# Delta rule, triangular inverse: odd chunks through the two other quarters of TensorE's array

## The reference, cut to what matters

```
def gated_delta_chunked(q, k, v, g, beta, s0):
    ...
    decay = jnp.exp(jnp.where(incl, g[..., :, None] - g[..., None, :], -jnp.inf))
    m = jnp.where(strict, jnp.einsum('bhnid,bhnjd->bhnij', k_beta, k) * decay, 0.0)
    t_inv = lax.linalg.triangular_solve(m + eye, ..., left_side=True, lower=True, unit_diagonal=True)
    u = jnp.einsum('bhnij,bhnjd->bhnid', t_inv, v * beta[..., None])
    w = jnp.einsum('bhnij,bhnjd->bhnid', t_inv, k_beta * jnp.exp(g)[..., None])
```

## Time and profile before

| | us |
|---|---|
| median of 3 runs | 4217.92 (4216.91 to 4218.13) |
| the profiled execution | 4220.12 |
| its span | 4218.3 |
| PE busy in the span | 3938.0 (93%) |
| DVE, ACT, POOL busy | 1680.2, 851.4, 692.3 |
| mean granted TensorE clock | 0.964 of full |

### The profile page before, as it was taken

The page is one execution under the profiler, slowest core; times in us unless marked ns, Lnnn a source line. Parts: engine busy times, 40 slices in busy tenths (PEclk is TensorE's granted clock), DMA queues, the critical chain, the costliest instruction groups (busy, mean ns, idle before and its releaser), DMA issues. The chain is left out here.

```text
span 4218.3 us, 51374 instructions
## 1 busy us (share of the span) xinstructions
PE 3938.0 (93%) x20867; PEld 2405.2 (57%) x20867; DVE 1680.2 (40%) x3134; ACT 851.4 (20%) x1663; POOL 692.3 (16%) x513
## 2 busy tenths in 40 slices
PE   7998889999999999899998999989998898999988
PEld 4565445554448666488745677768654444443333
DVE  2337343323764554533474656634124324111111
ACT  3224320000121333200013333321113201000000
POOL 0003212222420111123342332310002200000000
PEclk9999999999999999899998999999989998999999
DMA  5107611112541100254352010014200314999999
GB/s 175 40 11 285 198 40 60 60 60 95 170 126 56 46 31 26 93 217 160 111 173 50 26 31 26 19 39 154 63 0 1 155 46 192 406 420 422 422 421 374
DMA packets 323233, 580.12 MB, mean 138 GB/s; under 512 B 58700, under 2 KB 189228, under 8 KB 322360
## 3 DMA queue, kind: packets, MB, share of 16 engines
q1 hardware_dynamic: 323000, 576.83, 37.3%
...
## 5 line engine op out<-in xcount | busy, mean ns | idle before, releaser
L3348 PE MATMUL dn_ps<-room,dn_w 128*128 128x512 f32 (+1 forms) x616 | 230.2, 520 | 0.5 <-DVE dn_v_tok L3897 0.3
L961 PE MATMUL ffn_up_ps<-ffn_up_t,room 128*128 128x384 f32 (+1 forms) x704 | 208.3, 440 | 8.0 <-DVE room L1037 8.0
L961 PE MATMUL ffn_up_ps<-room 128*128 128x384 f32 (+1 forms) x704 | 203.9, 433 | 0.0
L4907 PE MATMUL experts_ps<-experts_ring,experts_xs 128*64 128x512 f32 (+1 forms) x768 | 164.1, 580 | 21.9 <-DMA experts_ring<-in_w_up 21.9
L961 PEld LDWEIGHTS ffn_up_ps<-ffn_up_t,room 128*128 128x128 f32 x704 | 136.0, 194 | 66.1 <-DVE room L1037 9.5
L1233 PE MATMUL ffn_down_ps<-ffn_down_w_sums,ffn_w 128*128 128x512 f32 x330 | 163.1, 604 | 10.8 <-DVE ffn_down_w_sums L1321 10.8
L2637 PE MATMUL hgrn_ps<-room,hgrn_w 128*128 128x512 f32 x372 | 170.3, 593 | 0.9 <-DVE hgrn_v L2891 0.9
L4907 PE MATMUL experts_ps<-experts_ring,room 128*64 128x512 f32 (+1 forms) x768 | 161.1, 570 | 8.7 <-DMA experts_ring<-in_w_up 8.1
L961 PEld LDWEIGHTS ffn_up_ps<-room 128*128 128x128 f32 x704 | 134.0, 190 | 55.5
L1044 DVE TENSOR_TENSOR room<-ffn_up_ps,room 128x384 f32<-128x384 f32 (+1 forms) x154 | 73.4, 489 | 222.2 <-PE ffn_up_ps L961 222.2
L5001 DVE TENSOR_TENSOR x_sb<-x_sb,experts_ps 128x512 f32<-128x512 f32 x56 | 38.5, 688 | 297.9 <-PE experts_ps L4842 297.9
...
## 6 DMA issues: line engine op xcount, KB each, us to landing
experts_ring<-in_w_gate SPq DMA_DIRECT2D x128, 704.0 KB, 14.9
experts_ring<-in_w_up SPq DMA_DIRECT2D x128, 704.0 KB, 16.7
...
```

Of the source, the lines that this page charges most:

```text
L961: mm = nc.tensor.matmul(result(n, p), lhs[:, k, :], rhs[:, k, :], start=k == 0, stop=k == half - 1)
L3348: mm = nc.tensor.matmul(out, ahead.tile[:, k, :] if k < by_ahead else wt[:, h % 2, piece, k, :], hT[:, k, tok], start=k == 0, stop=k == KD ...
L4907: mm = nc.tensor.matmul(ps[out_rows, 3 * n + c, 0:b - a], xs_now[:, j, at:at + SLOTS], ring[:, w_at + a:w_at + b], start=j == 0, stop=j == ...
```

## The change

`Y` is split by the chunk's parity. For odd chunks the output of `y` goes to the other half of the partitions, and `d` and `dt` read `Y` and `LT` from there, so that odd chunks use the upper right and lower left quarters. Their output comes back to the right half. Even and odd chunks write to different banks: `y` to 2 and 3, `d` and `dt` to 3 and 4 (three chunks each, `dt` behind `d` in the bank).

To have the odd chunks' `LT` in the other half, DVE makes it (`crossed`: two instructions per level, one for each half, reading `W` in one half and writing `LT` in the other), straight after `place_w`. POOL makes the even chunks' `LT` only, half as much. `y` now waits for `place_w` of the level before (`w_cp`), since it writes into bank 3. `place_z` waits for the end of `dt`, where it waited for the end of `d`, and `d`'s own semaphore is gone. The copies into `T` at level 5 are four where they were two.

```diff
-        Y = sb("Y", TILES, BLOCK)
+        Y = sb("Y", 2, ODD, BLOCK)
...
+        def split_of(bank, side, c, after=0):
+            return ps[sides_of[side], bank + c % 2, (after + c // 2) * BLOCK:(after + c // 2 + 1) * BLOCK]
+        def half_at(side, c):
+            return side if c % 2 == 0 else 1 - side
...
                 if n == 0:
                     pe.wait_ge(S["y_out"], L * h)
+                    pe.wait_ge(S["t_off"], 2 * h)
+                pe.wait_ge(S["w_cp"], (L - 1) * h + n)
...
-                        mm = nc.tensor.matmul(block_of(2, to_side, c), neg_m[rows, c, sides_of[to_side]], R[rows, c, :], start=True, stop=True)
+                        mm = nc.tensor.matmul(split_of(2, half_at(to_side, c), c), neg_m[rows, c, sides_of[to_side]], R[rows, c, :], start=True, stop=True)
...
-                if n < L - 1:
-                    for c in range(TILES):
-                        for side, rows in enumerate(sides_of):
-                            mm = nc.tensor.matmul(block_of(3, side, c), LT[rows, c, :], Y[rows, c, :], start=True, stop=True)
-                    mm.then_inc(S["d_mm"], 1)
+                pe.wait_ge(S["lt_crossed"], 2 * (L * h + n + 1))
                 pe.wait_ge(S["w_cp"], (L - 1) * h + n)
...
+                if n < L - 1:
+                    for i in range(ODD):
+                        for c in (2 * i, 2 * i + 1):
+                            for side in range(2):
+                                rows = sides_of[half_at(side, c)]
+                                nc.tensor.matmul(split_of(3, side, c), LT[rows, c, :], Y[rows, c % 2, c // 2, :], start=True, stop=True)
+                    for i in range(ODD):
+                        for c in (2 * i, 2 * i + 1):
+                            for side in range(2):
+                                rows = sides_of[half_at(side, c)]
+                                mm = nc.tensor.matmul(split_of(3, side, c, ODD), Y[rows, c % 2, c // 2, :], LT[rows, c, :], start=True, stop=True)
+                    mm.then_inc(S["dt_mm"], 1)
+                    return
...
-                nc.gpsimd.tensor_tensor(LT[:, :, :], W[:, h % 2, :, :], small(SMALL_HALVES + n + 1), ALU.mult).then_inc(S["lt_done"], 1)
+                nc.gpsimd.tensor_tensor(LT[:, 0::2, :], W[:, h % 2, 0::2, :], small(SMALL_HALVES + n + 1, ODD), ALU.mult).then_inc(S["lt_done"], 1)
...
-                dve.wait_ge(S["d_mm"], (L - 1) * h + n + 1)
-                nc.vector.copy_predicated(Z[:, :, :], small_mask(n + 1), blocks(3)).then_inc(S["z_cp"], 1)
+                dve.wait_ge(S["dt_mm"], L * h + n + 1)
+                nc.vector.copy_predicated(by_parity(Z[:, :, :]), parity_mask(n + 1), split_blocks(0)).then_inc(S["z_cp"], 1)
...
+            def crossed(n, h):
+                if h is None or n == L:
+                    return
+                if n:
+                    dve.wait_ge(S["w_cp"], (L - 1) * h + n)
+                else:
+                    dve.wait_ge(S["w_start"], 2 * h + 2)
+                    if h:
+                        dve.wait_ge(S["dt_mm"], L * h)
+                for side, rows in enumerate(sides_of):
+                    nc.vector.tensor_tensor(LT[sides_of[1 - side], 1::2, :], W[rows, h % 2, 1::2, :], small(SMALL_HALVES + n + 1, ODD, rows), ALU.mult).then_inc(S["lt_crossed"], 1)
...
                 place_w(n, hi)
+                if n < L - 1:
+                    crossed(n + 1, hi)
+                else:
+                    crossed(0, hp)
```

More of the change, by code:

```diff
@@ L3164, in chunk @@
         return slice(at, at + P)
+    ODD = TILES // 2
     sides = []
@@ L3247, in delta_mixer @@
                                              "conv", "z_cp", "r_done", "w_cp", "w_start", "kk_out", "mt_done", "qk_out", "ssq_out", "ssk_out", "v_scaled", "b_done", "q_scaled", "rho", "s_done",
[L3248 removed]
+                                             "o_half", "o_done", "w_ident", "lt_done", "lt_crossed", "rhs_done", "b_wide", "qk_masked", "t_done", "t_off", "stored", "z_in*2", "z_mm", "z_taken", "z_stored*4", also=[ahead.sem]))
         def wide(first):
@@ L3267, in block_of, with split_blocks, by_parity, parity_mask @@
             return ps[sides_of[side], bank, c * BLOCK:(c + 1) * BLOCK]
-        def small(n):
-            return cst[:, HALVES + n // 2, n % 2 * BLOCK:(n % 2 + 1) * BLOCK].unsqueeze(1).broadcast_to([P, TILES, BLOCK])
+        def split_of(bank, side, c, after=0):
+            return ps[sides_of[side], bank + c % 2, (after + c // 2) * BLOCK:(after + c // 2 + 1) * BLOCK]
+        def split_blocks(after):
+            return ps[:, 3:5, after * BLOCK:(after + ODD) * BLOCK].rearrange("p o (c i) -> p o c i", c=ODD)
+        def by_parity(x):
+            return x.rearrange("p (c o) i -> p o c i", o=2)
+        def parity_mask(level):
+            n = SMALL_EITHER + level
+            rows = cst[:, HALVES + n // 2, n % 2 * BLOCK:(n % 2 + 1) * BLOCK]
+            return rows.bitcast(U32).unsqueeze(1).unsqueeze(1).broadcast_to([P, 2, ODD, BLOCK])
+        def half_at(side, c):
+            return side if c % 2 == 0 else 1 - side
+        def small(n, count=TILES, part=slice(0, P)):
+            return cst[part, HALVES + n // 2, n % 2 * BLOCK:(n % 2 + 1) * BLOCK].unsqueeze(1).broadcast_to([part.stop - part.start, count, BLOCK])
         def small_mask(level, part=slice(0, P)):
@@ L3426, in d_of @@
                     pe.wait_ge(S["t_off"], 2 * h)
+                if n < L - 1:
[11 more added lines that the diff above has]
+                    return
                 for c in range(TILES):
-                    for side, rows in enumerate(sides_of):
-                        to_side = side if n < L - 1 else 1 - side
-                        mm = nc.tensor.matmul(block_of(4, to_side, c), Y[rows, c, :], LT[rows, c, :], start=True, stop=True)
+                    for side in range(2):
+                        rows = sides_of[half_at(side, c)]
+                        mm = nc.tensor.matmul(split_of(3, 1 - side, c), Y[rows, c % 2, c // 2, :], LT[rows, c, :], start=True, stop=True)
                 mm.then_inc(S["dt_mm"], 1)
@@ L3823, in place_w @@
                 for d, rows in enumerate(sides_of):
-                    nc.vector.tensor_copy(T[rows, h % 2, d, :, sides_of[1 - d]], blocks(4)[rows, :, :]).then_inc(S["t_off"], 1)
+                    for odd in range(2):
+                        ins = nc.vector.tensor_copy(T[rows, h % 2, d, odd::2, sides_of[1 - d]], ps[rows, 3 + odd, 0:ODD * BLOCK].rearrange("p (c i) -> p c i", c=ODD))
+                    ins.then_inc(S["t_off"], 1)
+            def crossed(n, h):
[9 more added lines that the diff above has]
+                    nc.vector.tensor_tensor(LT[sides_of[1 - side], 1::2, :], W[rows, h % 2, 1::2, :], small(SMALL_HALVES + n + 1, ODD, rows), ALU.mult).then_inc(S["lt_crossed"], 1)
             def rest(n, h):
```

7 lines of the change are left out of this document (3 added, 4 removed).

## The result

The changed kernel takes 4250.29 us in the median of 4 runs (4245.81 to 4252.88), the kernel before, timed beside it, 4218.02 (4216.91 to 4218.85): a ratio of 1.0076, 95% interval 1.0061 to 1.0091. The forecast was 4233, with 4212 to 4250. The direction was right and the size was not: +15 foreseen, +32 measured. The profiled execution is the fastest of the four (4245.81, span 4244.0) and shows 25.7 us of the difference in the span. All of it, and 1.4 us more, is in the stage of the delta rule.

What follows compares the result with a forecast made beforehand. PE was taken to set the pace, with DVE's slack thin. Waits of +1.2 us per full pass, +7 with the ends, plus +8 of clock gave +15 and 4233 us; own range 4224 to 4243, 8-in-10 range 4212 to 4250.

Steps and rivals of the forecast that it cites:

- the clock's term: PE idle ahead of `out_of` grows to about 2.5 us, clock falls: 1.5 us in each of passes 3 to 7, +8.
- Bursts: PE's bursts run in four quarters: `y` saves 0.34 us, `d` with `dt` 0.69, at most 47 us over eight heads.
- `crossed` at W+1.03: DVE's two products, POOL's `LT` between, end 1.03 us after `place_w` ends; next DVE instruction starts at 0.95.
- Steps 1 and 2: Periods 0 and 1: `carry` and `v_tok` come later behind `crossed`, delaying `out_of` and projection v; together +0.51 us.
- Step 3: Period 2: `y` of period 3 waits for `place_w` behind the convolution's step 3, +0.85 us; the 0.69 saving is lost.
- Step 4: Period 3: PE is alone, saves 0.34 and 0.69, ACT gives back about 0.14: -0.89 us; next `y` -0.34.
- Steps 4 to 6: Periods 3 to 5: next `y` -0.34; period 4 +0.54 from POOL collision and `place_w` wait; period 5 +0.50 ahead of `tr_of`.
- The ends: First and last passes, waits only: pass 1 +1.1 us, pass 2 0, pass 8 +0.3.
- A: Rival: the clock stays up, leaving only the waits' +7 us: 4225; chance 0.17.
- B: Rival: both crossed products run back to back without POOL: 4225 with the clock's loss, 4218 without; chance 0.10.
- C: Rival: quarters don't overlap by four, bursts stay as long, `place_z` comes 0.69 us later per level: 4260; chance 0.10.
- D: Rival: crossed products cost DVE little, free about 0.4 us after `place_w`, deciding at about 0.5: 4209; chance 0.08.

Runs made afterwards that it cites:

- wait_only: Kernel before, with only the new wait of `y` for `place_w` of the level before added: 4232.75 us, ratio 1.0030.
- clock_all: Changed kernel with unneeded matmuls filling PE's longer idle stretches, also in passes 1 and 8, waits kept: 4229.09 us, ratio 1.0023.
- before_filled: Kernel before, with unneeded matmuls filling PE's idle ahead of `ks_of` in pass 8 alone: 4216.56 us, ratio 0.9992.
- pool_waits: Changed kernel with POOL's `LT` waiting until both crossed products on DVE are done: 4241.79 us, ratio 1.0052.
- two_quarters: Changed kernel with odd chunks back in the even chunks' two quarters; waits, banks, order and DVE products stay: 4280.00 us, ratio 1.0144.

## Why the prediction fell short

The step that failed is the clock's term at the two ends of the stage. The prediction counted a loss of clock once in each of passes 3 to 7 and nothing elsewhere; passes 1, 2 and 8 stood in its sum with +1.1, 0 and +0.3 for waits alone. They came out at +5.5, +1.2 and +3.6, mostly by the clock. The steps of the middle pass held, as the list shows.

The median is 17 us over the forecast: 12 in the stage, less 1.4 outside it, and 6.7 because the profiled execution lies 4.5 under its median here and lay 2.2 over it before.

- **Bursts, 0.34 and 0.69 saved.** Right: 0.58 us in each.
- **`crossed` at W+1.03, the next DVE instruction at W+0.95.** Right: `place_w` ends at 2570.19, the pair at 2571.23, `carry` starts at 2571.16, W+0.97. The pair alone is 0.74 (taken: 0.65). `LT` at half size takes 0.59 alone (taken: 0.6) and 0.75 with its share of the turns.
- **Steps 1 and 2, +0.51 up to the projection v.** From the first `y` to v it took 16.06 us before and 18.35 now (2566.21 to 2584.56). 1.7 of this is the low stretch, so +0.6.
- **Step 3, +0.85.** v to `y` of period 3: 11.93 before, 12.87 now, +0.94. wait_only shows the cause by itself.
- **Step 4, -0.89.** `y` to `y` over period 3: 8.91 before, 8.06 now, -0.85.
- **Steps 4 to 6 behind it** (-0.34, +0.54, +0.50 by step). `y` of period 4 to that of period 5 takes 10.55, +0.42, more than the +0.20 of the two terms; and from there to `tr_of` 7.26 instead of 6.88, +0.38. `tr_of` comes at W+7.40 (W, the end of the first row below, is 2615.90); W+7.4 was forecast.

The last `place_w` of that pass and the first `y` of the next, after, in the timeline:

```profile
2615.32 0.58 DVE L3854 COPY_PREDICATED dn_W<-cst,dn_ps 128x384 f32<-128x384 uint32 x1
...
2635.03 0.58 PE L3435 MATMUL dn_ps<-dn_R,dn_neg_m 64*64 64x64 f32 x24
```

The starts of `y` in the kernel before, for these lengths (period 0, period 4, and period 0 of the next pass; the others stand in the earlier trace rows):

```profile
2553.85 0.92 PE L3411 MATMUL dn_ps<-dn_R,dn_neg_m 64*64 64x64 f32 x24
...
2590.75 0.45 PE L3411 MATMUL dn_ps<-dn_R,dn_neg_m 64*64 64x64 f32 x8
...
2619.49 0.68 PE L3411 MATMUL dn_ps<-dn_R,dn_neg_m 64*64 64x64 f32 x16
```

- **Sum per pass, +1.2.** 68.82 (2566.21 to 2635.03) less 1.7 for the low stretch less 65.64 is +1.5, and clock_all has +1.6. So the chain of the middle pass was right, 0.3 to 0.4 us short in all.
- **Clock +8, once in each of passes 3 to 7.** The place and the price (1.5, measured 1.7) were right. Pass 4 had two such stretches. Passes 3 to 7 grew by 16.8 us; 13.4 were forecast.
- **The ends: here the sum failed.** Pass 1 was put at +1.1, pass 2 at 0, pass 8 at +0.3, 1.4 together. They are 5.5, 1.2 and 3.6, 10.3 together: nine of the twelve us by which the stage of the profiled execution (+27.1) is over the forecast's +15. In pass 1 there is no recurrence, so in its first period nothing stands on PE between `dt` and the next `y`, and the new wait for `place_w` is bare. The timeline has it at once, and again at 2317.06 (1.09):

```profile
2305.98 0.53 PE L3458 MATMUL dn_ps<-dn_LT,dn_Y 64*64 64x64 f32 x24
2308.39 0.58 PE L3435 MATMUL dn_ps<-dn_R,dn_neg_m 64*64 64x64 f32 x24 [1.88 <-DVE dn_W L3854]
2308.90 5.41 PE L3370 MATMUL dn_ps<-room,dn_w 128*128 128x256 f32 x16
```

And the windows view right behind it:

```profile
2309.60:2313.00 3.40, 3.40 (x9) 2.72 (x9) 0.00 (x0) 0.00 (x0) 1.04 (x1) 0.50 0.00 0
```

- The waits by themselves aren't what the sum lost in pass 1: PE's idle time there goes from 0.9 to 6.8 us, by about the 5.8 that the bursts free. What it lost is the clock that fell behind them. The row above is a low stretch right behind the first wait. Pass 1 has three, 10 us, where there was none, at half speed a loss of 5.1 of its 5.5 us; and pass 8 has 24 us instead of 10. clock_all, with one low stretch left in pass 1 and none in pass 8, has +2.1 in the first and -1.9 in the last: 3.4 and 5.5 us less than the changed kernel. Not all of the 5.5 belongs to the change: before_filled's pass 8 is 4.7 us shorter than that of the kernel before. In pass 2 the clock stayed up, and its +1.2 are waits (wait_only alone has +1.5 there).
- **The range.** Its upper part came from the bounds of the steps and of the clock in the middle passes; the ends had none. The median, 4250.29, lies just above its end of 4250, and 7 us above that of the forecast's own range. The profiled execution, 4245.81, lay inside the wide one. The other three runs are 3.5 to 7.1 us slower, two of them at a mean granted clock lower by 0.001 and 0.002, which suggests that runs of one kernel differ in their low time. No term of the sum held that.
- **Rivals.** A, the clock staying up, is clock_all: 4229, where 4225 was priced. B's premise (back to back) holds only in pool_waits; in the changed kernel the turns were real. C was priced at 4260, two_quarters measures 4280: the same ends and the clock there were left out. D's turning point, W+0.5, wasn't reached: `carry` came at W+0.97.
